# Past attention with page pairs: where the column maximum stands, and where the last sequence's value tiles go

## What is computed

```
def _fox_attend(q, k, v, cum_q, cum_k, q_off):
        s = jnp.einsum('bqhd,bkhd->bhqk', q_i, k).astype(f32) * ATTN_SCALE
        s = s + jnp.transpose(cq_i, (0, 2, 1))[..., None] - cum_k_t[:, :, None, :]
        s = jnp.where(k_idx[None, None, None, :] <= pos_i[None, None, :, None], s, -jnp.inf)
        pr = jax.nn.softmax(s, axis=-1)
        return jnp.einsum('bhqk,bkhd->bqhd', pr.astype(v.dtype), v)
```

## Time and profile before

| | us |
|---|---|
| median of 3 runs | 2896.29 (2889.84 to 2897.46) |
| the profiled execution | 2893.86 |
| its span, first to last instruction | 2892.2 |
| granted TensorE clock, mean | 0.873 |
| FoX over the past, first key issue to last write of `yT` | 296 to 726 |
| dilated over the past, the same | 2066 to 2386 |

### The profile page before, as it was taken

How to read it: one execution, slowest core, us unless ns; L and a number is a source line. 1 busy time by engine, 2 the same in 40 slices (tenths; PEclk the granted TensorE clock), 3 DMA queues, 4 the chain that set the end, 5 groups by cost and what they waited for, 6 DMA issues and landing times. The chain is left out here.

```text
span 2892.2 us, 65333 instructions
## 1 busy us (share of the span) xinstructions
PE 2346.2 (81%) x26485; PEld 1811.4 (63%) x26485; DVE 1433.7 (50%) x2240; ACT 862.1 (30%) x1565; POOL 368.7 (13%) x566
## 2 busy tenths in 40 slices
PE   6778787875966897567999988977877767899998
PEld 3654576764733785255777766744566655677776
DVE  1325677773236451457552235256666655654223
ACT  1424344441213120023332222205533323333122
POOL 0002143433000000010110000032211111011000
PEclk9897789996976895688999999998988778899999
DMA  8220699997354101021332322351499972232331
GB/s 262 54 58 20 217 367 341 370 341 236 83 203 149 32 4 16 17 59 49 90 88 82 93 79 67 94 190 66 111 288 286 275 210 59 61 92 80 88 92 57
DMA packets 309814, 392.26 MB, mean 136 GB/s; under 512 B 26645, under 2 KB 227808, under 8 KB 309562
## 3 DMA queue, kind: packets, MB, share of 16 engines
q1 hardware_dynamic: 277274, 278.62, 31.2%
q0 software_dynamic: 32288, 110.12, 11.6%
HBM read 377.98 MB, written 10.70 MB: 134 GB/s over the span
## 5 line engine op out<-in xcount | busy, mean ns | idle before, releaser
L748 PE MATMUL bank<-yT,WH 128*128 128x288 f16 x3200 | 532.1, 290 | 44.5 <-DVE yT L611 34.2
L801 DVE SCALAR_TENSOR_TENSOR WL<-wring,WH 128x1024 f16<-128x1024 f32 x194 | 255.1, 1319 | 290.4 <-ACT WH L781 290.4
L748 PEld LDWEIGHTS bank<-yT,WH 128*128 128x128 f16 x3200 | 316.2, 99 | 130.5 <-issue 38.3
L1241 DVE TENSOR_TENSOR KL<-bank,KH 128x512 f16<-128x512 f32 x416 | 282.7, 687 | 194.3 <-ACT KH L1217 185.7
L1136 PE MATMUL bank<-cst,kslot 128*128 128x128 f32 x1664 | 303.2, 311 | 78.6 <-DMA kslot<-in_cache_fox_k 43.0
L1217 ACT CAST KH<-bank 128x512 f16<-128x512 f32 x416 | 241.7, 585 | 387.8 <-PE bank L1136 387.8
L748 PE MATMUL bank<-uT,WH 128*128 128x288 f16 x2048 | 337.9, 288 | 11.0 <-DVE WL L801 11.0
L748 PE MATMUL bank<-yT,WL 128*128 128x288 f16 x1600 | 331.4, 289 | 0.0
L781 ACT ACTIVATE WH<-wring 128x1024 f16<-128x1024 f32 x194 | 203.4, 1053 | 320.0 <-PE bank L748 221.0
L1136 PEld LDWEIGHTS bank<-cst,kslot 128*128 128x128 f32 x1664 | 198.6, 155 | 106.2 <-DMA kslot<-in_cache_fox_k 50.5
L748 PEld LDWEIGHTS bank<-uT,WH 128*128 128x128 f16 x2048 | 201.4, 98 | 63.6 <-issue 11.6
(11 more groups left out here) (400 smaller groups left out, 3671.4 us busy)
## 6 DMA issues: line engine op xcount, KB each, us to landing
kslot<-in_cache_fox_k SPq DMA_DIRECT2D x256, 256.0 KB, 5.3
vslot<-in_cache_fox_v POOLq DMA_DIRECT2D x256, 256.0 KB, 5.3
wring<-in_ada_w SPq DMA_DIRECT2D x96, 512.0 KB, 5.1
kslot<-in_state_dil_k SPq DMA_DIRECT2D x80, 512.0 KB, 10.2
vslot<-in_state_dil_v POOLq DMA_DIRECT2D x80, 512.0 KB, 13.8
wring<-in_mlp_up SPq DMA_DIRECT2D x64, 512.0 KB, 4.1
wring<-in_mlp_down SPq DMA_DIRECT2D x64, 512.0 KB, 3.9
wring<-in_ev_w_in SPq DMA_DIRECT2D x26, 512.0 KB, 3.8
```

The source lines that it names most:

```text
L748: last = nc.tensor.matmul(bank[b + h][:, 0:HALF], w[s % 2][:, c, :], x[:, s % parts * KC + c, h * HALF:(h + 1) * HALF], start=(s % parts = ...
L801: nc.vector.scalar_tensor_tensor(WL[s % 2][:, :, :], w[:, :, :], WSCALE, WH[s % 2][:, :, :], ALU.mult, ALU.subtract).then_inc(w_free, 1)
L1241: nc.vector.tensor_tensor(KL[i][:, :], turned[n % NT][:, :], KH[i][:, :], ALU.subtract).then_inc(lo_out, 1)
```

## The change

It does three things in `attend_past`, for both stages.

- POOL takes the column maximum of a sequence ahead of its value tile 7 instead of ahead of tile 2: after tiles 0 to 6.
- In the last sequence, value tiles 8 to 11 (dilated: 8 and 9) go to the four key slots, once their last keys are turned, and are issued by SP behind its last keys. TensorE reads them there.
- FoX's tiles 12 to 15 of the last sequence go to the value slots of that sequence's tiles 0 to 3, once these are used: 12 and 14 issued by POOL, 13 and 15 by SP, which signal on semaphores of their own (`late`).

```
...
+            LAST = NT_ - nt
...
+            late = {x: sem(f"v_late{x}") for x in range(VR + KR, nt) if x % 2 == 1}
+
+            def v_home(t):
+                x = t - LAST
+                if VR <= x < VR + KR:
+                    return K[x - VR], k_in[x - VR], LANDED * (NT_ // KR + 1)
+                if x >= VR + KR:
+                    t -= VR + KR
+                    if x in late:
+                        return V[t % VR], late[x], LANDED
+                    return V[t % VR], v_in[t % VR], LANDED * (t // VR + 2)
+                return V[t % VR], v_in[t % VR], LANDED * (t // VR + 1)
+
+            def take_v(eng, t):
+                x = t - LAST
+                if VR <= x < VR + KR:
+                    eng.wait_ge(kt_ok, (NT_ - KR + x - VR + 1) * TU)
+                elif x >= VR + KR:
+                    eng.wait_ge(v_used, used_up_to(t - VR - KR))
+                elif t >= VR:
+                    eng.wait_ge(v_used, used_up_to(t - VR))
+                dst, landed, _ = v_home(t)
+                load_v(eng, t, dst, landed)
...
                         load_k(sp, t, K[t % KR], k_in[t % KR])
+                    for x in range(VR, nt):
+                        if x < VR + KR or x in late:
+                            take_v(sp, LAST + x)
...
-                        if t % nt == 2:
+                        if t % nt == VR - 1:
...
-                        if t >= VR:
-                            pool.wait_ge(v_used, ((t - VR + 1) * TU + SG - 1) // SG)
-                        load_v(pool, t, V[t % VR], v_in[t % VR])
+                        x = t - LAST
+                        if x < VR or (x >= VR + KR and x not in late):
+                            take_v(pool, t)
...
-                            pe.wait_ge(v_in[t % VR], LANDED * (t // VR + 1))
+                            rows, landed, value = v_home(t)
+                            pe.wait_ge(landed, value)
...
-                                                        V[t % VR][:, 512 * part + j * P:512 * part + (j + 1) * P], start=(u == 0), stop=False, skip_group_check=E > 1)
+                                                        rows[:, 512 * part + j * P:512 * part + (j + 1) * P], start=(u == 0), stop=False, skip_group_check=E > 1)
```

More of the change, by code:

```diff
@@ L1106, in attend_past, with used_up_to @@
             slots = N + VLAG
+            LAST = NT_ - nt
+            assert NT_ % KR == 0 and nt >= VR
+            def used_up_to(t):
+                return ((t + 1) * TU + SG - 1) // SG
+            late = {x: sem(f"v_late{x}") for x in range(VR + KR, nt) if x % 2 == 1}
[19 more added lines that the diff above has]
+                load_v(eng, t, dst, landed)
             with nc.Block() as block:
```

## The result

| | before | after |
|---|---|---|
| median, us | 2895.47 (6 runs) | 2877.88 (6 runs, 2868.66 to 2888.58) |
| ratio, 95% interval | | 0.9947 (0.9923 to 0.9970) |
| the profiled execution, us | 2893.86 | 2868.66 |

The change is faster, by 15 us by the ratio (9 to 22 by its interval) or 18 by the medians, where 32 was forecast. The profiled execution of after is the fastest of its six, so its 25 us against the one of before say too much. That is scatter.

What follows compares the result with a forecast made beforehand. No engine was full; FoX's middle was close to four limits, its tail bound by POOL's issue rate, the dilated stage by transfers. Terms 23 - 1 + 2 - 1 + 2 + 7 = 32 us took 2896.3 to 2864, range 2842 to 2885.

Steps and rivals of the forecast that it cites:

- step 2: FoX turns: tile 6 issued first makes the maximum about 0.3 us late, 2 us over seven, 1 us at the last.
- step 3: FoX middle: filling the turn's hole gains 4 us, 2 net of the late maximum; the stage's start loses 1.
- step 4: Dilated middle: filling the turn's hole gains 12 us, five tiles ahead cost 10.4; gain 2, between +12 and -10.
- Step 1: FoX tail after the last maximum: 17 us instead of 39.8, gain 23, the main term.
- the other term, the loads: FoX tail: value loads land 11.7 us after the maximum, so the last group cannot end before 13.6.
- rival B: Both stages: prefetched values push keys back, costing 6.5 us in FoX and 10 in dilated; 2887 us, chance 0.12.
- Rival C: POOL waits for value slots while the maximum is ready; three tiles late at eight turns, 2919 us, chance 0.04.
- Step 5: Dilated tail after the last maximum: 11.7 us instead of 18.7, gain 7.
- a FoX period above 49: Sign of being wrong in the FoX middle, pointing to late maxima or delayed keys; 47 to 48 us was expected.
- DVE waiting for the maximum more than 1 us a turn: Sign of being wrong at the turns, pointing to POOL standing before value slots while the maximum is ready.

Runs made afterwards that it cites:

- one queue: The changed kernel with the maximum ahead of value tile 5 and POOL issuing every value tile, SP keys alone; ratio 0.9982 to the kernel before, median 2887.4 us.
- the repeat: The changed kernel timed once more with no edit, as reference for the others; ratio 0.9934 to the kernel before, median 2878.7 us.
- At 8: The changed kernel with the column maximum ahead of value tile 8 instead of 7; ratio 0.9997 to the kernel before, median 2898.0 us.
- the kernels at 6: The changed kernel with the maximum ahead of tile 6 in both stages (2862.0 us), and the same but ahead of tile 2 for the first dilated sequence (2870.6 us).
- the rows at 5: Five variants of the changed kernel with FoX's maximum ahead of tile 5, differing in queues or dilated place; ratios 0.9869, 0.9982, 0.9937, 0.9909 and 0.9934 to before.

## Why the prediction was wrong

The sign was right and the size was twice what came: 32 us forecast, 14.6 in the two stages. The tails gave 3.3 us more than was taken. What failed lies before the last maximum of each stage: FoX was forecast to break even there and lost 11.5 us (steps 2 and 3), the dilated stage was forecast to gain 2 and lost 7.2 (step 4). That is 9.2 us for step 4, 3.8 for step 2, 3.0 for step 3 with the start, and 4.7 that stay open.

*Step 1, the FoX tail: right, its size partly by luck.* 17 us forecast, 16.4 and 16.5 measured, gain 23.4 for 23. That the issues behind the maximum were what was short is shown: with one queue the tail is 32.8. But the 17 was eight groups at the low clock, 15.3 us. The granted clock was 0.50, 0.73 and 1.00 in the three 4 us from 692 on, and the first six groups took 7.1 us. The tail ended by the other term, the loads, which was put at 13.6: the last group starts 14.5 us after the maximum (707.34) where 11.7 was worked out. POOL's wait of 3.4 us that no semaphore explains (last section) is in it.

*Step 2, the late maximum: the term that was mis-sized.* The mechanism was named, with its place and the pieces in its way, and sized at 0.3 us in the middle and 1 at the end, 3 us in all. The eight turns were late by 6.8 us more than before, and 6.8 in the repeat. Two terms were too small. First, from the end of the value group to the end of the second issue I took 2.3 us, twice an issue's distance; the rows show 1.25 us from the group's end (443.56) to the first issue's start (444.81), so 2.9 to the second's end, and a lateness of 0.76. Second, at the last turn the group ran for 1.91 us instead of 1.07 and ended 0.4 us ahead of the input instead of 2.2, which made 2.54.

The last FoX maximum stands 11.5 us later after the stage's first load (repeat: 10.1). Counted one for one, the lateness is 6.8 of them. At 8 it is 25.0 of 27.9. That leaves 4.7, 3.3 and 2.9 us, no more than the 5.3 and 6.8 by which the kernels at 6 stand later with nothing late, so no run shows that a microsecond of lateness costs more than one. Whether what is left is scatter (the rows at 5 span 7.5 us) or keys pushed back (S, rival B) stays open. Rival C, put at 0.04, is the same mechanism with three late tiles; here one was late.

*Step 3, FoX middle: the gain did not come.* I took 4 us for filling the turn, and 1 lost at the start. In the six kernels with the maximum at 4 or 5, which load two or three tiles more ahead of the turn and are never late, the periods are 47.3 to 48.7, none clearly below the old 47.6. So filling the hole gave nothing measurable. The start's 1 us cannot be told either: the first maximum came 51.7 us after the first load, 53.6 in the repeat, 52.1 before.

*Step 4, dilated middle: the step that failed most.* Forecast a gain of 2, 12 for the turn's hole less 10 for the tiles ahead; the last maximum came 7.2 us later (repeat 8.3). The hole was there and was filled, but the six periods gained 2.0 us (repeat 1.7) instead of 12. Two things were wrong in it: the hole of one turn was taken for all six, and a share of 0.77 was read as idle capacity, in a stage that moved its bytes at 276 to 290 GB/s in every kernel, with shares from 0.99 to 1.02. The cost side held: 10.4 us forecast, and the first maximum came 6.6 us later (repeat 7.9). The seventh period, 2.6 us longer, makes up the rest. Here rival B was right.

*Step 5, dilated tail: right and low.* 8.8 and 8.3 us for the 11.7 taken, gain 9.9 for 7. By the timeline of PE in the changed kernel, four groups took 5.79 us and the last 1.05, less than 1.91 each:

```profile
2345.85 5.79 PE L1212 MATMUL bank<-vslot,ST 128*16 128x128 f32 x128 [3.74 <-ACT ST L1257]
2351.47 1.05 PE L1212 MATMUL bank<-kslot,ST 128*16 128x128 f32 x32
```

The gain is that of the maximum's place and not of the second queue: with both queues and the maximum at 2 this tail is 18.0.

So 23.4 + 9.9 - 11.5 - 7.2 = 14.6, against 15 by the ratio. Two signs of being wrong came: a FoX period above 49 (49.1, repeat 49.0), and DVE waiting for the maximum more than 1 us a turn, 7.6 us over seven turns. Five of these seven waits are 0.7 us, one is 1.2 and the last 3.1.

## What to carry to other kernels

An operation that others wait for belongs in a queue ahead of every entry whose own wait ends near it: not only busy time counts, but the last wait in front. Here moving it one tile forward was worth 17 us by the medians, as much as the whole change had brought, though the traces show only 8 of them in the two stages. The safe place could be read off beforehand, ahead of the tile whose slot is freed by the turn itself. In a stage bound by its bytes, loading ahead mostly moved time from the end to the start; it paid by what it took off the tail, 9.9 us here for 7.2.

## What the runs showed of the hardware that was not expected

The mean share of the DMA engines and their rate came apart: 0.99 and 1.02 of the time busy, and 282 GB/s in both, in the same stage with the same tiles. Other kernels' six periods had 284 GB/s at 0.99 (maximum at 5) and 280 at 1.02 (the repeat). A share short of 1 was no measure of what could be added.

A FoX transfer issued by POOL costs its queue 1.15 us while it runs through and 1.8 from the end of the value group that it waits for to the first issue's end (443.56 to 444.81 + 0.54). The first issue after such a wait should be counted by the second number.

POOL stands idle for 3.4 us ahead of its 131st and its 245th transfer of the program, in all 14 traces and wherever the maximum stands; in the changed kernel the 245th is the first piece of tile 14, the last tile that POOL loads in FoX:

```profile
699.05 0.54 POOL L1519 DMA_DIRECT2D vslot<-in_cache_fox_v  x1 [0.60 <-PE bank L1212]
702.98 0.54 POOL L1519 DMA_DIRECT2D vslot<-in_cache_fox_v  x1 [3.39 <-issue]
```

No semaphore explains it. SP's last tile waits for the same value group and was issued by 702.17, before POOL's began. In the changed kernel TensorE then waited 2.07 us for tile 14; by that row the pause cost it about 2 us (an estimate). The kernel before has the same idle time in its tail (3.38 us, at 701.93), so its 28 pieces were not one per 1.15 us throughout. The cause was not tried.
